# Where the normalising of the softmax stands in VectorE's order of a two-layer attention stage

## The reference

```python
# for each head of each unit: q, k of 64 rows (plus 32 rotated rows in the mla units), 256 keys
scores = (q @ k.T) * scale + mask        # causal; for "dil" units three dilated windows share one softmax
p = softmax(scores, axis=-1)             # for "sel" units the mask also keeps the top-k keys of an index score
o = p @ v
```

## Time and profile before

| What | Value |
|---|---|
| Median of 3 runs | 1587.94 us |
| Profiled execution, its own time | 1587.94 us |
| Its span in the profile | 1586.2 us |
| TensorE matmul, busy | 1322.8 us (83%), 7712 instructions |
| VectorE, busy | 468.6 us (30%) |
| ScalarE, busy | 296.3 us (19%) |
| Chain that ended last | PE 64%, DMA 28%, DVE 5%, issue 1%, ACT 1% |

### The profile page before, as it was taken

One profiled execution on the slowest core, in us unless ns is written; L12 is line 12 of the kernel. 1 busy time (PEld: TensorE's weight loads), 2 busy tenths in 40 slices (PEclk: granted clock), 3 DMA queues, 4 the chain that ended last, 5 costly groups with the idle time before them and its releaser, 6 DMA issues.

```text
span 1586.2 us, 18796 instructions
## 1 busy us (share of the span) xinstructions
PE 1322.8 (83%) x7712; PEld 750.5 (47%) x7712; DVE 468.6 (30%) x1108; ACT 296.3 (19%) x616; POOL 0.2 (0%) x4
## 2 busy tenths in 40 slices
PE   6999999956756656589999999756999999998658
PEld 4565788412311212167767743321577677443213
DVE  5225463101101101013664522210235645221102
ACT  2422211100000000022322312200223233122002
POOL 0000000000000000000000000000000000000000
PEclk9999999988788888799999999977999999998889
DMA  9475388999999999993521499999915224999994
GB/s 383 176 265 213 113 333 350 406 428 427 426 428 428 427 428 428 428 426 135 213 106 54 165 388 384 408 420 419 424 58 212 85 75 160 370 380 402 424 421 205
DMA packets 39390, 492.50 MB, mean 311 GB/s; under 512 B 4352, under 2 KB 4736, under 8 KB 5888
## 3 DMA queue, kind: packets, MB, share of 16 engines
q1 hardware_dynamic: 39152, 491.06, 75.2%
q10 hardware_dynamic: 144, 0.13, 0.0%
HBM read 490.13 MB, written 1.05 MB: 310 GB/s over the span
## 4 chain that ended last, share of the span: by engine, by line
PE 64%; DMA 28%; DVE 5%; issue 1%; ACT 1%; SPq 0%; DVEq 0%; ACTq 0%
PE PS L662 21%; DMA A<-ring_d 19%; DMA A<-ranked_d 9%; PE PS L1616 7%; PE PS L1026 4%; PE PS L1460 4%; PE PS L1599 4%; PE PS L1643 3%; PE PS L667 3%; PE PS L966 2%; PE PS L1581 2%; PE PS L1684 2%; PE PS L1250 1%; PE PS L1670 1%; PE PS L734 1%
## 5 line engine op out<-in xcount | busy, mean ns | idle before, releaser
L662 PE MATMUL PS<-A 128*128 128x256 f32 (+4 forms) x1552 | 363.5, 392 | 4.3 <-DVE A L2105 1.0
L1026 PE MATMUL PS<-A 128*32 128x512 f32 x1472 | 219.2, 733 | 133.7 <-DMA A<-ring_d 133.5
L662 PEld LDWEIGHTS PS<-A 128*128 128x128 f32 x1552 | 272.6, 194 | 87.4 <-issue 50.5
L1026 PEld LDWEIGHTS PS<-A 128*32 128x32 f32 x1472 | 49.8, 123 | 290.7 <-issue 234.3
L1616 PE MATMUL PS<-A 128*32 128x512 f32 (+1 forms) x768 | 116.8, 695 | 76.5 <-DMA A<-ranked_d 76.5
L1616 PEld LDWEIGHTS PS<-A 128*32 128x32 f32 (+1 forms) x768 | 33.1, 130 | 150.2 <-issue 150.2
L2170 DVE TENSOR_TENSOR A<-A,PS 128x512 f32<-128x512 f32 x8 | 5.5, 688 | 316.6 <-PE PS L1026 316.6
L1643 PE MATMUL PS<-A 128*32 128x512 f32 (+1 forms) x512 | 80.2, 596 | 0.8 <-issue 0.8
L2681 DVE TENSOR_TENSOR A<-A,PS 128x256 f32<-128x256 f32 x22 | 9.3, 422 | 234.5 <-ACT A L3236 234.5
L667 PEld LDWEIGHTS PS<-A 128*128 128x128 f32 (+1 forms) x396 | 46.2, 146 | 47.7 <-issue 26.8
L667 PE MATMUL PS<-A 128*128 128x128 f32 (+1 forms) x396 | 59.7, 283 | 10.8 <-DVE A L2170 7.1
(11 more groups left out here) (405 smaller groups left out, 1300.7 us busy)
## 6 DMA issues: line engine op xcount, KB each, us to landing
A<-ring_d SPq DMA_DIRECT2D x155, 2048.0 KB, 25.4
A<-ranked_d SPq DMA_DIRECT2D x48, 2048.0 KB, 12.3
A<-ranked_d SPq DMA_DIRECT2D x48, 1024.0 KB, 19.8
A<-ring_d SPq DMA_DIRECT2D x2, 1312.0 KB, 27.9
A<-ring_d SPq DMA_DIRECT2D x2, 1280.0 KB, 23.7
A<-p_d SPq DMA_DIRECT2D x1, 1152.0 KB, 31.2
A<-xT_d SPq DMA_DIRECT2D x1, 1024.0 KB, 5.5
A<-cT_d SPq DMA_DIRECT2D x1, 1024.0 KB, 11.9
```

The costliest lines, as they stand in the source:

```text
L662: ins = g.matmul(out, l, r, start=n == 0, stop=n == len(pairs) - 1)
L1026: ins = g.matmul(ps[32 * e:32 * e + 32, :], rows_of(kk, e), wv[4 * (kk % 2) + e], start=kk == 0, stop=kk == 7)
```

## The change

Only `head_steps` is changed, so the same steps come in another order. `nr` of unit t-1 no longer stands between `sc` and `sm` of unit t, but directly ahead of `tr` of unit t-1. In turn 0, `sm` now stands ahead of the front step, as in all other turns.

```diff
     for t in range(len(units) + 2):
+        if t < len(units):
+            out += [("sc", *units[t]), ("sm", *units[t])]
         front, behind = among[t]
-        now = [("sc", *units[t])] if t < len(units) else []
-        softmax = [("sm", *units[t])] if t < len(units) else []
-        if t:
-            out += now + ([("nr", *units[t - 1])] if t <= len(units) else []) + softmax + front
-        else:
-            out += now + front + softmax
+        out += front
         pair = t > 1 and units[t - 2][0] == "dil"
         if pair and units[t - 2][1] % 2:
             out.append(("pv", *units[t - 2]))
         if 0 < t <= len(units):
-            out.append(("tr", *units[t - 1]))
+            out += [("nr", *units[t - 1]), ("tr", *units[t - 1])]
         out += behind
```

## The result

The changed kernel takes 1596.85 us in the median of five runs (1594.79 to 1598.14), before 1587.94 us; the ratio is 1.0059, with a 95% interval of 1.0036 to 1.0083, or 5.7 to 13.2 us slower. The forecast was 1595.7 us. The profiled execution took 1596.44 us with a span of 1594.6 us, 8.4 us more than before.

The account below looks back on a forecast made before the run. TensorE was taken to bound the mixer, its delays passing on one for one. Terms of 1.54 - 0.79 + 1.72 + 0.64 + 0.76 = +3.87 us a layer, +7.74 for two, gave 1595.7 us from 1587.94; range 1591 to 1600 us.

Parts of the forecast that it names:

- Turn 0, raw copy behind the exponentials: First rotation on TensorE waits for a raw copy now behind four exponentials on ScalarE: +1.54 us a layer (1.5 to 2.8).
- Turns 1 to 5: The 7 us projection between scores and transposes covers the later normalising on VectorE: 0.
- Turn 6: Softmax moves up, normalising makes transposes late, yet the rotation starts earlier: -0.79 us a layer (-1.24 to +1.09).
- Turn 7, behind the pair's copy: Normalising of `sel` 0 queues behind the `dil` pair's copy, so transposes start late: +1.72 us a layer (1.5 to 1.9).
- Turn 8: Transposes wait for normalising behind the maxima; the output product in between is half as long: +0.64 us a layer.
- Turn 9: Transposes wait for normalising behind the maxima, with a shorter output product in between: +0.76 us a layer.
- Turn 10: It has no softmax and keeps its order: 0.
- The path from the maxima to the transposes: Turns 6, 8, 9: 0.02 issue, 0.19 reciprocal to multiply, 1.03 or 1.14 multiply, 0.05 handoff to TensorE, in us.
- The table load at nothing: Turn 0, ScalarE: the 1.28 us table load runs in idle time without waiting for its activation's input, adding nothing.
- That rival: Turn 0's table load waits for the maxima and stands in the chain: +1.28 us a layer, 1598.3 us; chance 0.09.
- the vanishing stalls: Rival: the short stalls of turns 8 and 9 vanish, leaving 2.47 us a layer, 1592.9 us; chance 0.06.
- the absorbing stream: Rival: the expert stage's weight stream absorbs the mixer's delay, time stays at 1587.9 us; chance 0.07.

Follow-up runs that it names:

- the three experiments: Kernel before with new order in turn 0 alone, 1.0032; in turn 6 alone, 0.9988; changed kernel with turn 7's normalising ahead of the pair's copy, 1.0021.
- the longer filler: Kernel before with 27 instead of 9 filler matmuls on TensorE behind the mixer in both layers: 1599.95 us against 1586.45, ratio 1.0081.
- the version with the raw copy first: Kernel before with turn 6's raw copy ahead of the exponentials on ScalarE, VectorE's order kept: 1583.71 us against 1586.45, ratio 0.9972.
- Turn 0 alone: Kernel before with the new order in turn 0 only, exponentials ahead of the raw copy: 1592.00 us against 1586.45, ratio 1.0032.
- the change with turn 7 mended: Changed kernel with turn 7's normalising ahead of the pair's copy, still behind softmax: 1590.41 us against 1586.67 for the kernel before, ratio 1.0021.
- the filled turn 0: Kernel before with turn 0's new order and 5 filler matmuls in TensorE's wait ahead of the first rotation: 1591.00 us against 1586.12, ratio 1.0039.
- the changed kernel timed again: Changed kernel, same list built by other code, against the kernel before on the same chip: 1597.59 us against 1586.12, ratio 1.0073.

## Why the prediction was right

Each term is the difference between two starts on TensorE in the changed kernel, less the same difference before, layer 1:

| Step | Forecast | Measured | From |
|---|---|---|---|
| Turn 0, raw copy behind the exponentials | +1.54 | +1.54 | start of softmax 0 to rotation: 3.93 less 2.39 |
| Turns 1 to 5 | 0 | +0.01 | first rotation to that of turn 5: 54.32 less 54.31 |
| Turn 6 | -0.79 | -0.76 | rotation of turn 5 to rotation: 11.77 less 12.53 |
| Turn 7, behind the pair's copy | +1.72 | +1.76 | rotation to transposes: 16.32 less 14.56 |
| Turn 8 | +0.64 | +0.62 | transposes to transposes: 11.46 less 10.84 |
| Turn 9 | +0.76 | +0.77 | the same: 8.65 less 7.88 |
| Turn 10 | 0 | +0.03 | transposes to transposes: 6.07 less 6.04 |
| Sum | +3.87 | +3.97 | |

The start of softmax 0 before is 764.71 (the row before the first of the earlier trace rows). The sum for two layers, 7.94 us, is the bulk of the measured difference. Turns 0, 6 and 7 have experiments of their own. Turns 8 and 9 have none: what the three experiments leave of the 3.95 us of the first mixer is 3.95 - 1.55 + 0.86 - 1.82 = 1.44 us, against 1.39 in the table.

*Two readings were off,* and neither shows in the sum. The path from the maxima to the transposes was put together with 0.02 us ahead of the reciprocal and 0.05 for the handoff to TensorE. In turns 6, 8 and 9 the reciprocal starts 0.07 to 0.08 us ahead of the end of the maxima's row, and from the end of the multiply to the transposes pass 0.14 to 0.15 us in all four turns. The two errors cancel, by luck; in turn 7, where there is no gap behind maxima, copy to transposes takes 1.72 us instead of 1.60, of which 0.07 is made up by the pair's product, which follows the rotation that much sooner. And the chain of before does not stay on TensorE behind the mixer: it runs on VectorE for the router, from 892.16 to 897.58 us. Since that work waits for TensorE too, it moves with it, and the delay still passes on.

*The table load at nothing* was right: rows 4 had shown that such a load does not wait, and it ran at 757.74. That rival is ruled out; so are the vanishing stalls, since turns 8 and 9 gave 0.62 and 0.77, and the absorbing stream, by the longer filler. By the Trainium skill, page "ScalarE: Activation LUTs", section "What ACT_TABLE_LOAD costs", a switch costs a drain on top of the load; here neither could matter, as 5.67 us of idle time lay behind the load.

*What the sum left out* in the profiled execution is the granted clock. That execution divides so: ahead of the first mixer -1.46 us (nothing is changed there, yet over the thirteen profiles this stretch takes 754.70 to 761.74 us, a large part of the runs' spread), mixers +3.95 and +5.54, first expert stage -0.22, the rest +0.6, in all 8.4 us. The second mixer holds 1.59 us of lowered clock beside its 3.95. The two falls behind the routers cost 1.68 each at the place. Of the first about 1.2 stay: from router to second layer the six profiles with such a fall take 298.5 us in the mean, the seven without 297.3, though single ones of the two groups overlap (297.91 and 298.13).

*How much of the time the change owes to the clock* stays open. Over all profiles, an empty wait of 2.3 us ahead of the first rotation was followed by a fall 3 times in 10, all in the second layer; a wait of 0.78 us never in 12, a filled one never in 4. The longer filler's fall came behind the wait of 1.73 us in turn 6 of the second layer, the only one behind ten waits of that kind. Behind the router falls came 9 times in 26, also in the version with the raw copy first, which is the fastest. Turn 0 alone costs 5.5 and 4.9 us in time for 3.1 us of mixer, but the change with turn 7 mended, which has the same turn 0, costs only 3.7 for 4.3. The intervals allow the mixers' 3.1 for turn 0 alone and 4.3 for the change with turn 7 mended. They do not reach down to the mixers' share for the filled turn 0 (4.0 to 8.2 us, mixers 3.0), nor for the changed kernel timed again (9.4 to 13.8 us, mixers 7.9): there the mixers as profiled do not account for the whole time, and no run shows what does.

The mean granted clocks of the executions do not settle it. Turn 0 alone averages 0.9289 (12 executions) against 0.9290 for the kernel before on the same chip (29), and the changed kernel timed again 0.9296 (5) against 0.9297 (11): no lower clock where the time is 2.4 and 3.6 us above the mixers' share. The filled turn 0 averages 0.9282 (6) against the same 0.9297. A fall that costs 1.6 us lowers the mean of one execution by about 0.001 (an estimate: 1.6 of 1586 us), and single executions of before lie between 0.921 and 0.936, so one such fall more or less is within the scatter.

## What to carry to other kernels

When one list sets the order on several engines, look for what is queued behind a step, not at the step: the multiply of turn 7 stood ready while VectorE was idle for 9.55 us, held by a copy in front of it whose input came from the very engine that waited. Moving the later user's work behind the earlier user's work adds no instruction and can be worth the wait in full; in turn 6 one raw copy put ahead of four exponentials gave 1.9 us a layer. A swap that looks symmetric is to be priced turn by turn, since it is paid for only where the bounding engine has nothing else to do in between.

## What the runs showed of the hardware

The granted clock of TensorE can fall to the 1.2 GHz level in a stage where it is busy for 95% of the time (151.00 of 159 us from 1181 to 1340 us of the changed kernel's profile), after idle stretches of 2.3, 1.7 or only 0.66 and 0.49 us. In the same place of the same list it falls in one execution and not in the next, and costs 1.6 to 3.2 us at the place. The Trainium skill, page "TensorE: Matmul & The Clock Gate", section "Part 1: The HAM clock gate", ties the clock to how busy the engine has lately been and calls it variable from run to run how many matmuls run slowly. The traces agree in the second: the places of the falls differ between executions. For the first they show only that all 13 falls in the mixers and behind the routers came behind idle stretches, most of which pass without one. A new wait of 2.3 us thus cost its length and, in 3 of 10 cases, 1.6 to 3.2 us more; behind the new waits of 0.5 to 1.8 us in turns 6 to 9 none is seen.
